# First block of the input projection: its modulation by TensorE, chunks 0 and 1 in two transfers each, conditioning vector asked for ahead of the tokens

## The reference

```python
x = layer_norm(x, ln_in_g, ln_in_b)
c_act = silu(c)
mod = c_act @ w_ada + b_ada              # 6 x 1024 columns
sh1, sc1, gt1, sh2, sc2, gt2 = split(mod, 6)
h = x * (1 + sc1) + sh1
proj = h @ w_in                          # 1024 -> 1952 columns
# latent attention, retention, w_out, norm, ffn; then the second block with
# delta rule, stick-breaking attention and 32 experts
```

## Time and profile before

| | |
|---|---|
| median of 3 runs | 930.15 us (929.66 to 932.19) |
| profiled execution, its own time | 931.34 us |
| its span, first to last instruction | 929.5 us |
| PE busy | 886.2 us, 95% |
| DVE, ACT, POOL busy | 39%, 19%, 10% |
| moved from and to memory | 218.65 MB read, 237 GB/s over the span |

### The profile page before, as it was taken

One profiled execution on the slowest core, in us unless ns is written; L12 is line 12 of the kernel. 1 busy time (PEld: TensorE's weight loads), 2 busy tenths in 40 slices (PEclk: granted clock), 3 DMA queues, 4 the chain that ended last, 5 costly groups with the idle time before them and its releaser, 6 DMA issues.

```text
span 929.5 us, 11962 instructions
## 1 busy us (share of the span) xinstructions
PE 886.2 (95%) x4905; PEld 549.1 (59%) x4905; DVE 363.7 (39%) x837; ACT 177.2 (19%) x363; POOL 90.8 (10%) x90
## 2 busy tenths in 40 slices
PE   6999799999999998999999999999999999999984
PEld 3446756766667764688868878577455333333321
DVE  5736816433223338364276321563255111101004
ACT  3126512100000000321341221241021111101001
POOL 0045302301011110300000000000020000000000
PEclk9999999999999999999999999789999999999998
DMA  9997847543334445034254114002897999999993
GB/s 371 428 422 287 342 202 276 222 180 149 134 132 167 194 200 202 1 100 171 91 193 155 30 80 158 24 8 91 344 377 245 370 398 423 421 421 425 418 415 126
DMA packets 24653, 218.30 MB, mean 235 GB/s; under 512 B 3657, under 2 KB 3937, under 8 KB 10002
## 3 DMA queue, kind: packets, MB, share of 16 engines
q1 hardware_dynamic: 21330, 205.76, 55.7%
q0 software_dynamic: 3264, 11.72, 3.5%
HBM read 218.65 MB, written 2.10 MB: 237 GB/s over the span
## 4 chain that ended last, share of the span: by engine, by line
PE 83%; DVE 5%; DMA 5%; SPq 3%; ACT 2%; issue 1%; DVEq 0%; POOLq 0%; ACTq 0%
PE psum L2373 12%; PE psum L2395 9%; PE psum L512 8%; PE psum L467 6%; PE psum L2161 6%; PE psum L1406 6%; DMA scr<-in_gates 3%; PE psum L771 3%; PE psum L2354 3%; PE psum L2133 3%; PE psum L1461 3%; PE psum L1430 3%; PE psum L2105 2%; PE psum L591 2%; SPq L2015 1%
## 5 line engine op out<-in xcount | busy, mean ns | idle before, releaser
L2373 PE MATMUL psum<-hT,ring 128*128 128x256 f32 x512 | 115.4, 379 | 1.1 <-issue 1.1
L2373 PEld LDWEIGHTS psum<-hT,ring 128*128 128x128 f32 x512 | 97.1, 190 | 26.7 <-issue 14.2
L512 PE MATMUL psum<-hT,ring 128*128 128x272 f32 x320 | 74.2, 393 | 0.0
L512 PEld LDWEIGHTS psum<-hT,ring 128*128 128x128 f32 x320 | 60.6, 190 | 12.9 <-issue 0.5
L1406 PE MATMUL psum<-ring,hT 128*32 128x512 f32 (+1 forms) x240 | 56.7, 594 | 3.0 <-DMA scr<-in_gates 3.0
L2395 PE MATMUL psum<-scr 128*128 128x512 f32 x128 | 59.5, 592 | 0.0
L2834 DVE TENSOR_TENSOR scr<-ring 128x512 f32<-128x512 f32 x16 | 11.1, 691 | 121.6 <-PE psum L2395 121.6
L467 PE MATMUL psum<-hT,ring 128*128 128x256 f32 x256 | 58.1, 383 | 0.0
L2161 PE MATMUL psum<-ring,hT 128*128 128x512 f32 (+1 forms) x128 | 54.0, 585 | 2.1 <-ACT hT L2466 2.1
L467 PEld LDWEIGHTS psum<-hT,ring 128*128 128x128 f32 x256 | 47.7, 190 | 6.8 <-issue 0.2
L1802 DVE TENSOR_TENSOR scr<-psum,scr 128x256 f32<-128x256 f32 x11 | 4.7, 424 | 120.1 <-ACT scr L1575 120.1
(11 more groups left out here) (553 smaller groups left out, 1273.0 us busy)
## 6 DMA issues: line engine op xcount, KB each, us to landing
ring<-in_stream SPq DMA_DIRECT2D x54, 2048.0 KB, 9.1
ring<-in_gates SPq DMA_DIRECT2D x9, 2048.0 KB, 23.6
ring<-in_downs SPq DMA_DIRECT2D x14, 1024.0 KB, 20.8
scr<-in_gates SPq DMA_DIRECT2D x6, 2048.0 KB, 26.4
scr<-in_gates SPq DMA_DIRECT2D x8, 1024.0 KB, 28.5
scr<-in_downs SPq DMA_DIRECT2D x8, 1024.0 KB, 16.1
scr<-in_stream SPq DMA_DIRECT2D x3, 2048.0 KB, 18.7
rowB<-in_rows POOLq DMA_DIRECT2D x5, 1024.0 KB, 12.3
```

Of the source, the lines that this page charges most:

```text
L512: last = mm(psum[:, g % 4, 0:L2], w[:, k, m * P:(m + 1) * P], hT[:, k, :], start=(k == 0), stop=(k == KD - 1))
L2373: last = mm(psum[:, f if f < 4 else 0, 0:NT], w[:, k, m * P:(m + 1) * P], hT[:, k, META:L2], start=(k == 0), stop=(k == KD - 1))
```

## The change

- SP issues `crow`, `ident`, X, `col` in this order instead of X, `ident`, `crow`, `col`.
- Chunks 0 and 1 are moved in two transfers each: first the w_ada part (1 MB), which counts up a semaphore of its own (`mod_landed`), then the w_in part.
- The w_ada part of chunk 0 is laid out untransposed, as sixteen 128 x 128 matrices, two sums of eight. TensorE multiplies them with `csil` (silu of c as columns, 128 x 8): sixteen matmuls with one moving column into bank 6. Ahead of them it makes eight matmuls of the identity with itself into bank 7. All of this stands between the `cB` matmuls and the transposes, in TensorE's order.
- DVE no longer reduces block 0; it reads the two sums from PSUM.
- ACT makes `csil` first of all, ahead of the square roots. It applies A1 and B1 to block 0 as it takes it from PSUM (two pieces of 128 columns), and copies the other blocks behind that.
- TensorE's block 0 takes the column groups in the order 3, 2, 1, 0 and waits for ACT's copies before group 1, whose banks the transposes used. `hk` counts one more.
- DVE's block 1 waits for the first half of chunk 1 only.

```diff
         def landed_wait(eng, n):
-            eng.wait_ge(landed[slots[n]], sum(16 * transfers(m) for m in range(n + 1) if slots[m] == slots[n]))
+            mods = 16 if slots[n] >= WHOLE else 0
+            eng.wait_ge(landed[slots[n]], mods + sum(16 * transfers(m) for m in range(n + 1) if slots[m] == slots[n]))
...
+            sp.dma_start(crow, IN["c_row"]).then_inc(S.in_cst, 16)
+            sp.dma_start(C("ident"), IN["consts"][:, 0:P]).then_inc(S.in_cst, 16)
             sp.dma_start(X[:, :, :], IN["x"].rearrange("(t p) d -> p t d", p=P)).then_inc(S.in_x, 16)
-            sp.dma_start(C("ident"), IN["consts"][:, 0:P]).then_inc(S.in_cst, 16)
-            sp.dma_start(crow, IN["c_row"]).then_inc(S.in_cst, 16)
...
+                if n in (AT["head"], AT["head"] + 1):
+                    sp.dma_start(ring_at(n)[:, 0:2 * DM], IN["stream"][n][:, 0:2 * DM]).then_inc(mod_landed(n), 16)
+                    sp.dma_start(ring_at(n)[:, 2 * DM:], IN["stream"][n][:, 2 * DM:]).then_inc(landed[slots[n]], 16)
...
             last.then_inc(S.cb_mm, 1)
+            for _ in range(8):
+                mm(psum[:, 7, 0:P], C("ident"), C("ident"), start=True, stop=True)
+            pe.wait_ge(S.silu_c, 1)
+            pe.wait_ge(mod_landed(AT["head"]), 16)
+            for i in range(2):
+                for k in range(KD):
+                    a = (i * KD + k) * P
+                    last = mm(psum[:, 6, i:i + 1], ring_at(AT["head"])[:, a:a + P], csil[:, k:k + 1],
+                              start=(k == 0), stop=(k == KD - 1))
+            last.then_inc(S.cb_mm, 1)
             transposes(1)
...
-                pe.wait_ge(S.hk, k + 1)
-                for c in PROJ_ORDER:
+                pe.wait_ge(S.hk, k + 2 if k else 1)
+                for c in PROJ_ORDER if k else (3, 2, 1, 0):
+                    if k == 0 and c == 1:
+                        pe.wait_ge(S.hk, 2)
...
+            act.wait_ge(S.in_col, 16)
+            nc.scalar.activation(csil, V("c"), ACT.Silu).then_inc(S.silu_c, 1)
             ln_sqrt(1, 0)
             ln_sqrt(1, 1)
             act.wait_ge(S.cb_mm, 1)
             nc.scalar.activation(cB, psum[:, 4:6, :].rearrange("p a b -> p (a b)"), ACT.Silu).then_inc(S.silu_c, 1)
-            act.wait_ge(S.in_col, 16)
-            nc.scalar.activation(csil, V("c"), ACT.Silu).then_inc(S.silu_c, 1)
+            act.wait_ge(S.mod1, 1)
             for t in range(T):
                 act.wait_ge(S.xn_tr, tr_count(1, t))
+                last = nc.scalar.activation(hT[:, 0, tok(t)], psum[:, 2 * t, 0:P], ACT.Identity, bias=B1[:, 0:1],
+                                            scale=A1[:, 0:1])
+            last.then_inc(S.hk, 1)
+            for t in range(T):
                 for half in range(2):
-                    ins = nc.scalar.copy(hT[:, 4 * half:4 * half + 4, tok(t)],
-                                         b_(2 * t + half).rearrange("p (k n) -> p k n", n=P))
-            link(ins)
+                    first = 1 - half
+                    ins = nc.scalar.copy(hT[:, 4 * half + first:4 * half + 4, tok(t)],
+                                         psum[:, 2 * t + half, first * P:512].rearrange("p (k n) -> p k n", n=P))
+            ins.then_inc(S.hk, 1)
+            act.wait_ge(S.hk, 2)
...
-            modulate(0)
             modulate(1)
...
-                landed_wait(dve, n)
-                for i in range(2):
+                if k == 1:
+                    dve.wait_ge(mod_landed(n), 16)
+                elif k:
+                    landed_wait(dve, n)
+                for i in range(2 if k else 0):
...
-                link(v.tensor_tensor(modc[:, k:k + 9:8], modc[:, k:k + 9:8], V("b_ada")[:, k:k + 9:8], ALU.add))
+                sums = modc[:, k:k + 9:8] if k else psum[:, 6, 0:2]
+                link(v.tensor_tensor(modc[:, k:k + 9:8], sums, V("b_ada")[:, k:k + 9:8], ALU.add))
...
-            dve.wait_ge(S.silu_c, 1)
             dve.wait_ge(S.in_col, 16)
+            dve.wait_ge(S.cb_mm, 2)
             modulation(0)
+            dve.wait_ge(S.silu_c, 2)
             modulation(1)
```

More of the change, by code:

```diff
@@ L1928, in transfers, with mod_landed @@
             return len(parts(n))
+        def mod_landed(n):
+            return landed[WHOLE + n - AT["head"]]
         def landed_wait(eng, n):
-            eng.wait_ge(landed[slots[n]], sum(16 * transfers(m) for m in range(n + 1) if slots[m] == slots[n]))
+            mods = 16 if slots[n] >= WHOLE else 0
+            eng.wait_ge(landed[slots[n]], mods + sum(16 * transfers(m) for m in range(n + 1) if slots[m] == slots[n]))
         @block.sync
         def _(sp):
+            sp.dma_start(crow, IN["c_row"]).then_inc(S.in_cst, 16)
+            sp.dma_start(C("ident"), IN["consts"][:, 0:P]).then_inc(S.in_cst, 16)
             sp.dma_start(X[:, :, :], IN["x"].rearrange("(t p) d -> p t d", p=P)).then_inc(S.in_x, 16)
-            sp.dma_start(C("ident"), IN["consts"][:, 0:P]).then_inc(S.in_cst, 16)
-            sp.dma_start(crow, IN["c_row"]).then_inc(S.in_cst, 16)
             sp.dma_start(col[:, :], IN["cols"]).then_inc(S.in_col, 16)
@@ L1995, in _ @@
                     sp.wait_ge(S.affine, 4)
-                if n < FIXED_END:
+                if n in (AT["head"], AT["head"] + 1):
+                    sp.dma_start(ring_at(n)[:, 0:2 * DM], IN["stream"][n][:, 0:2 * DM]).then_inc(mod_landed(n), 16)
+                    sp.dma_start(ring_at(n)[:, 2 * DM:], IN["stream"][n][:, 2 * DM:]).then_inc(landed[slots[n]], 16)
+                elif n < FIXED_END:
                     for words, a, b in parts(n):
@@ L2177, in proj_tail @@
                             landed_wait(pe, AT["head"] + k)
-                        pe.wait_ge(S.hk, k + 1)
+                        pe.wait_ge(S.hk, k + 2)
                         last = proj(k, c, t)
@@ L2916, in lay_out @@
         r = slice(n * P, (n + 1) * P)
-        stream[AT["head"] + n, :, 0:DM] = ada[:, r].T
-        stream[AT["head"] + n, :, DM:2 * DM] = ada[:, DM + n * P:DM + (n + 1) * P].T
+        if n == 0:
+            stream[AT["head"], :, 0:2 * DM] = np.stack([ada[:, 0:P], ada[:, DM:DM + P]]) \
+                .reshape(2, KD, P, P).transpose(2, 0, 1, 3).reshape(P, 2 * DM)
+        else:
+            stream[AT["head"] + n, :, 0:DM] = ada[:, r].T
+            stream[AT["head"] + n, :, DM:2 * DM] = ada[:, DM + n * P:DM + (n + 1) * P].T
         stream[AT["head"] + n, :, 2 * DM:2 * DM + 1952] = w[r]
```

## The result

| | before | after |
|---|---|---|
| median (20 runs each, taken together) | 930.27 us | 931.84 us |
| lowest and highest | 925.88, 932.83 | 927.35, 937.21 |
| ratio, 95% interval | | 1.0034 (1.0018 to 1.0050) |
| profiled execution, its own time | 931.34 us | 935.87 us |
| its span | 929.5 us | 934.1 us |

By the ratio the change costs 0.3%, some 3.2 us (1.7 to 4.7): on the 930.15 of the prediction that is 933.3. Forecast was 930.1, no difference, and a range of 928.3 to 932.9: 933.3 lies 0.4 above its top. The page of after differs little: TensorE is busy for longer and the clock's row begins with a 7.

The account below looks back on a forecast made before the run. TensorE, busy 95%, was taken as the bound, with block 3 held until ACT's input. Slack 0.75 against 0.7 us of later transfers gave -0.05, so 930.1 us from the median 930.15; range 928.3 to 932.9.

Parts of the forecast that it names:

- The pitch of 0.43 at full rate: Input projection on TensorE: 0.43 us per pass at once, making blocks 0 to 2 take 19.65 us.
- but at full rate from its first pass: Projection start on TensorE: between 15.4 and 16.4 us, middle 15.9, against 15.63, with no slow passes.
- B: TensorE's front: one-column matmuls or transposes run slow; start 17.1 to 19.9, +0.3 to +2.7 us; chance 0.14.
- C: TensorE's front: added work slow throughout, then a slow projection start; start 21.7, +6.1 us, 936.2; chance 0.07.
- The cap at 36.04: Projection block 3: cannot start before 36.04 us, when ACT has its input ready; 36.74 with the later transfers.
- the slack of 0.75: Projection block 3: 0.75 us between its possible start at 36.04 and its start at about 36.8.
- the forecast's -0.05: Start of projection block 3: 36.74 after the change against 36.8, so -0.05 us for the whole kernel.
- The shift s = 0.7 (0 to 0.9): First transfers: X and everything behind it, chunk 2 too, come 0.7 us later (0.88 less 0.16).
- Rival D, dearer halves: Split transfers: each extra one adds 1.7 us, chunk 2 up to 3.4 later; +3.3 us, 933.5; chance 0.03.
- Rival E: Block 3's limit gives way and TensorE's 1.25 us comes through; 928.3 to 928.9, at best -2.8; chance 0.10.
- ident at 3.3: First transfers: crow and ident land at 3.3 us, against 6.2 as the upper bound.
- Edits at nothing: Front: ACT's csil, table load and remaining copies, DVE's new wait, GpSimd's constants and SP's extra transfers cost nothing.

Follow-up runs that it names:

- the three of after: The changed kernel's first profile and two more without edit; projection starts 18.50, 21.39 and 18.30 us; a further ten-run set gave 935.1 us, ratio 1.0045.
- 3: The changed kernel with 32 moving columns instead of one in the modulation matmuls; one profile, 937.03 us.
- 4: The changed kernel without its eight identity matmuls; projection from 21.01 us, end 73.62; no whole time or ratio given.
- 2: The changed kernel with 128 moving columns instead of one in the modulation matmuls; 931.34 us, ratio 1.0011 over ten runs to the kernel before.
- 5: The changed kernel with 128 moving columns, its eight identity matmuls replaced by four of 512 columns ahead of cB; one profile, 926.54 us.
- 8: GpSimd's 1.3 MB of constants asked for behind chunk 3, but for early columns; on top of 7 ratio 0.9979, on top of 2 0.9960 and 0.9991.
- the second profile of before: The kernel before profiled again without edit; projection from 15.62 to 69.04 us, block 3 at 36.07.
- 7: The kernel before with two 512-column identity matmuls in TensorE's wait behind the transposes; ratio 0.9961, repeat 0.9969.
- 6: The kernel before with transfer edits alone: new order, ratio 1.0004; chunks 0 and 1 in halves, 1.0017; both, one profile without ratio.

## Why the prediction was wrong, by its own steps

- *The pitch of 0.43 at full rate, and "but at full rate from its first pass": this step failed.* The one-column passes were taken at 3.4 us with seven microseconds of unbroken matmuls ahead of them as the reason, and everything behind them at the fast level. So the cost of the transposes and of the first part of the projection was taken at half of what it came to. The one-column passes did begin fast in the first profile (a rise at 9.8 us), but in their course the clock fell, and the transposes took 3.53 us for 1.75, the projection five slow microseconds. In the second profile and with 32 columns the clock hadn't risen before the projection. Transposes behind one or 32 columns were slow in five profiles of five (the three of after, 3 and 4), behind 128 columns fast in five of five (2 twice, 5, 8 twice). Told apart by the rate before: where it was low ahead of these passes, it stayed low through one or 32 columns in three of three (the second of after, 3, 4) and rose within the 128-column passes in three of three (2 twice, 8 once); where it had risen before, it fell in the one-column passes in two of two (the first and third of after) and stayed up with 128 in two of two (5, 8 once). By what rule it falls or rises isn't shown; 4 is a rise behind narrow passes alone. The row at hand, the router's 16 one-column passes in 1.70 us, showed their cost within warm work, not what 32 of them leave behind.
- *The Trainium skill* ("TensorE: Matmul & The Clock Gate", What's actually happening) lets the clock follow how busy the engine has been recently. The windows above have TensorE busy 2.00 us of 2.00 ahead of the fall, so by the busy share that the profile shows the trace doesn't agree with it.
- *Rivals B and C had the mechanism.* B (start 17.1 to 19.9, +0.3 to +2.7) is the first and third profile by its start, 18.50 and 18.30, and C (21.7, +6.1) the second, 21.39: end of the projection +6.46 on 69.67. They had 0.14 and 0.07, too little. What spoke for them stood in the prediction: 3.7 us of `cB` and the transposes behind it never reached the fast level. B's size missed the slow start of the projection, 2.5 us more (55.10 less 52.61): its +2.7 is 19.9 + 19.65 - 36.8, with blocks 0 to 2 at full rate, although its condition was slow passes just ahead of them.
- *The cap at 36.04: right; the slack of 0.75 was 0.66.* The last five blocks take 32.97 us at full rate, not the 32.75 of 5 x 6.55, so in the earlier trace rows block 3 began at 69.67 - 32.97 = 36.70, not at 36.8; the forecast's -0.05 would have been +0.04. The cap showed as 36.07 in the second profile of before, 36.16 and 36.29 in 7, always with ACT as releaser; and with the constants moved ACT came at 34.24.
- *The shift s = 0.7 (0 to 0.9): the term was mis-sized.* X came 1.4 us later. The order alone gives 0.96 of that: issued 0.84 later, and the 0.16 us to be won back weren't (5.27 us from issue to landing, against 5.15). Order and halves together gave 1.24, and over all profiles with both X came 1.0 to 1.5 later. Chunk 2 came 2.1 later, of which 0.9 is order and halves. So no version of the change with GpSimd's constants where they were reached the -0.05: at full rate throughout, block 3 started at 36.92 in 5 (end of the projection 0.2 us behind 69.67), and at 38.17 and 38.47 in 2 (1.5 and 1.8 behind), where the prediction had 36.74.
- *Rival D, dearer halves:* 0.3 us at chunk 2, not 3.4. By an estimate from the Trainium skill ("DMA: Bandwidth & Descriptors", Bandwidth) the halves would have taken 2.4 us longer, as the prediction has it; the trace doesn't agree. The section's advice is to batch to 1 MiB and more, which the halves still are, so, other than the prediction says, it doesn't speak against them.
- *Rival E:* its "-2.8 with every term at its best" is given without its terms and can't be followed.
- *ident at 3.3: right,* 3.16 (1.98 after its issue at 1.18). The two pieces of ACT took 0.46 each against 0.4. `csil` was there at 7.82, and neither it nor its table load is on the chain.
- *Edits at nothing:* ACT, which waited for `mod1` and the transposes at 16.26 and 17.90, had copied the rest by 20.1, and the column groups 1 and 0 weren't held up for it in the chain.
- *Behind the front:* the shift went through, +3.94 at 73.61. A further 0.75 came at about 107 to 117 us, where the granted clock falls in both kernels (0.67 from 108 to 112 us before; 0.61 from 108 to 112 and 0.54 from 112 to 116 after), 1.6 were given back in the delta rule, and 1.4 came behind it; the profiled run ended 4.5 us later. All three vary from profile to profile of one kernel.

The result, 3.2 us (1.7 to 4.7), lies below the front of all three profiles of after (+3.8 to +6.5 on 69.67) and above that of 2 (+1.5 to +1.8). The base explains a part only of the gap: before's own front ended at 69.04 or 69.67, and by 72 in the versions of 6 with a slow start. That the whole is a mixture of executions with and without a low clock at the front, and with the slow delta-rule stretch in some, is argued; how often each occurs wasn't counted.

## What to carry to other kernels

A matmul that loads 128 x 128 weights for one column keeps TensorE busy in the profile and can yet leave it at 1.2 GHz for what follows (from 13.4 to 23.5 us here); price what follows at half rate, or give the matmul 128 moving columns, which cost at most 0.3 us for 32 passes here (3.7 us, against 3.4 by the earlier trace rows). Where TensorE waits for its first large stage, two dense matmuls of the identity in that wait are the cheapest edit tried here and the only one that gained twice; the projection was at full rate from its first pass in all three profiles that have them, but most of the 3 us gained isn't explained by the front. And when work is taken off a path, look up what is late next (here a transfer, 0.66 us behind) before pricing the gain: the reductions that were removed stood ahead of a cap that the change could only push back.

## What the runs showed of the hardware that was not expected

- The granted clock fell from 1.00 to 0.50 at 13.4 us with TensorE busy without a break, and rose at 23.5, behind 5 us of 512-column passes.
- The clock's column says 1.00 at the start, where the pitch says half rate: four passes of 512 columns took 3.78 us there, and 1.98 in 5. In the second profile of after it says 1.00 up to the rise at 25.7 us too.
- 32 passes with full weight loads took the same at the slow level with 1 column and with 32 (6.83 and 6.88 us). At the fast level they took 3.7 to 3.8 us with 128, where 1 column would take 3.4 by the earlier trace rows: the columns hardly count.
- A small transfer alone (64 KB, issued at 1.18) landed 1.98 us later.
- The delta-rule stretch takes 85.75 us in nine of the eighteen profiles, and 90.3 or 91.9 in the other nine, in versions of either kernel; in the first profile of before the granted clock is 0.60 and 0.55 from 590 to 610 us. The difference, 4.5 to 6.1 us, is more than the whole effect studied.
